# A mixture-of-experts trunk layer on one Trainium2 core: TensorE's sequencer is told of the next expert's far body in every near body

## What is computed

```python
def grouped_moe(h, router_w, router_b, w_gate, w_up, w_down):
    t = h.reshape(-1, D)
    logits = (t @ router_w).astype(jnp.float32) + router_b
    aff = jax.nn.softmax(logits, axis=-1)
    ...                      # best group of four experts, top 2 inside it
    for e in range(N_EXPERTS):                       # 16
        hid = jax.nn.silu(t @ w_gate[e]) * (t @ w_up[e])     # 2048 -> 1024
        y = y + combine[:, e:e + 1] * (hid @ w_down[e])      # 1024 -> 2048
```

## Time and profile before

| what | value |
| --- | --- |
| median of 3 runs | 1832.25 us (1832.04 to 1832.47) |
| the profiled execution: its own time | 1831.08 us |
| the profiled execution: its span | 1829.4 us |
| mean granted TensorE clock over the span | 0.978 |
| the experts' part | from about 815 us to about 1805 us of the span |

### The profile page before, as it was taken

How to read it: one execution, slowest core, us unless ns; L and a number is a source line. 1 busy time by engine, 2 the same in 40 slices (tenths; PEclk the granted TensorE clock), 3 DMA queues, 4 the chain that set the end, 5 groups by cost and what they waited for, 6 DMA issues and landing times.

```text
span 1829.4 us, 22863 instructions
## 1 busy us (share of the span) xinstructions
PE 1696.8 (93%) x9430; PEld 1001.4 (55%) x9430; DVE 610.4 (33%) x1082; ACT 186.0 (10%) x439; POOL 362.6 (20%) x161
## 2 busy tenths in 40 slices
PE   6889998999999999969999989999988989899996
PEld 5668887878888878654443233343423324334322
DVE  0453648687676342441121120211111111211114
ACT  0000112100001100041010010010100101001000
POOL 0014740167677768300000000000000000000000
PEclk9889999999999999989999999999999999999999
DMA  9996886486788744434689998999999999899995
GB/s 386 425 388 176 366 365 256 190 332 287 316 352 341 303 165 203 184 140 185 277 368 418 428 425 373 427 425 427 427 427 428 427 428 428 359 428 423 429 427 215
DMA packets 51015, 629.92 MB, mean 344 GB/s; under 512 B 5775, under 2 KB 8240, under 8 KB 11848
## 3 DMA queue, kind: packets, MB, share of 16 engines
q1 hardware_dynamic: 49768, 623.15, 82.1%
q10 hardware_dynamic: 1120, 5.00, 0.7%
HBM read 624.46 MB, written 3.67 MB: 343 GB/s over the span
## 4 chain that ended last, share of the span: by engine, by line
PE 71%; DMA 19%; DVE 6%; SPq 1%; issue 1%; ACT 0%; DVEq 0%; ACTq 0%
PE bank L1396 24%; PE bank L858 20%; PE bank L870 9%; DMA ring<-in_w_up_gate 7%; PE bank L1158 7%; DMA region_g<-in_w_up_gate 6%; PE bank L1234 4%; PE bank L829 3%; DMA ring<-in_w_down 3%; PE bank L882 2%; DVE ada_rows L1912 2%; DMA region_g<-in_w_down 2%; DMA ring<-in_w_in 1%; PE bank L877 1%; SPq L584 1%
## 5 line engine op out<-in xcount | busy, mean ns | idle before, releaser
L858 PE MATMUL bank<-ring,region_b 128*64 128x512 f32 x1792 | 409.9, 604 | 42.2 <-DMA ring<-in_w_up_gate 34.5
L729 POOL TENSOR_TENSOR ring<-ring 128x1024 f32<-128x1024 f32 x152 | 360.2, 2396 | 356.4 <-DMA ring<-in_w_in 237.4
L858 PEld LDWEIGHTS bank<-ring,region_b 128*64 128x64 f32 x1792 | 124.5, 138 | 296.4 <-issue 244.8
L870 PE MATMUL bank<-ring,region_f 128*64 128x512 f32 (+1 forms) x1408 | 231.7, 518 | 8.9 <-DMA ring<-in_w_down 8.9
L1396 PE MATMUL bank<-ring,region_a 128*128 128x256 f32 x768 | 174.3, 385 | 4.7 <-DVE region_c L2106 4.2
L1396 PE MATMUL bank<-ring,region_x 128*128 128x256 f32 x768 | 170.2, 379 | 0.0
L1396 PEld LDWEIGHTS bank<-ring,region_a 128*128 128x128 f32 x768 | 147.7, 193 | 27.8 <-issue 6.9
L870 PEld LDWEIGHTS bank<-ring,region_f 128*64 128x64 f32 (+1 forms) x1408 | 77.0, 127 | 145.7 <-issue 116.9
L1396 PEld LDWEIGHTS bank<-ring,region_x 128*128 128x128 f32 x768 | 145.6, 190 | 19.3
L2339 DVE TENSOR_TENSOR region_a<-bank,region_a 128x512 f32<-128x512 f32 x128 | 79.5, 683 | 199.2 <-PE bank L882 199.1
L1912 DVE SCALAR_TENSOR_TENSOR bank<-ring,condT,bank 128x512 f32<-128x512 f32 x190 | 143.4, 755 | 5.7
(11 more groups left out here) (233 smaller groups left out, 1304.8 us busy)
## 6 DMA issues: line engine op xcount, KB each, us to landing
ring<-in_w_up_gate SPq DMA_DIRECT2D x112, 2048.0 KB, 22.2
ring<-in_w_down SPq DMA_DIRECT2D x56, 2048.0 KB, 20.8
ring<-in_ada_w SPq DMA_DIRECT2D x44, 2048.0 KB, 11.8
ring<-in_w_in SPq DMA_DIRECT2D x31, 2048.0 KB, 13.7
region_g<-in_w_up_gate SPq DMA_DIRECT2D x16, 2048.0 KB, 26.0
ring<-in_w_branch SPq DMA_DIRECT2D x8, 2048.0 KB, 14.6
ring<-in_w_out SPq DMA_DIRECT2D x8, 2048.0 KB, 9.8
region_g<-in_w_down SPq DMA_DIRECT2D x8, 2048.0 KB, 19.3
```

The lines of the kernel that those rows point to most:

```text
L729: ins = pool.tensor_tensor(quarter(s, *out)[:, k:k + 4, :], quarter(s, *in0)[:, k:k + 4, :], quarter(s, *in1)[:, k:k + 4, :], op)
L858: last = nc.tensor.matmul(bank_of(x, j)[n * c:n * c + n, 0:2 * m], tokens(x, 8 * half + k), w[:, k % 4, :, m * c:m * c + m], start=(half = ...
L870: last = nc.tensor.matmul(bank_of(x, q)[n * c:n * c + n, 0:m], hidT[x][:, k, :], w[:, k % 4, m * c:m * c + m], start=(k == 0), stop=(k == ...
```

## The change

An announcement is now emitted in the small body of *every* expert but the last, at the same place in the body, and every branch into a large body but the first is tied to the one in the small body ahead of it:

```diff
@@ -1131,8 +1131,8 @@
                 extra("F")(x)
                 if len(xs) > 2:
                     extra("add F")(x)
-            if not xs and le == GRP - 1 and not last_turn:
-                large_announced[g + 1] = pe.mark_branch_hint_location()
+            if not xs and ne < NE - 1:
+                large_announced[ne + 1] = pe.mark_branch_hint_location()
             down(0, 1, first).then_inc(half_used, 1)
             if 0 < len(xs) < 3:
                 extra("add F")(1)
@@ -1533,7 +1533,7 @@
                         e = expert_at(g, le)
                         count = pe.value_load(counts[0:1, e:e + 1], min_val=0, max_val=T)
                         here = few_tokens(pe, f"pe{g}_{le}", count, lambda xs: expert_pe(pe, mm, g, le, xs),
-                                          large_announced.get(g) if le == 0 else None)
+                                          large_announced[g * GRP + le])
                         asked.append((g, le, count, here))
```

## The result

| | kernel before | changed kernel |
| --- | --- | --- |
| median of 7 runs each | 1832.04 us (1829.18 to 1832.64) | 1840.75 us (1835.44 to 1841.93) |
| ratio | | 1.0049 (95% interval 1.0040 to 1.0058) |
| the profiled execution: its own time | 1831.08 us | 1840.70 us |
| its span | 1829.4 us | 1839.0 us |
| fetches on queue 8 | 88 | 98 |

The change makes the kernel slower, by 8.7 us or 0.5%. The forecast was 1.5 us slower, within what can be told from no change, and a range that ended at 1836.3. The measured time lies outside it.

A forecast was written before the change was run, and what follows sets the result against it. Weights set the pace in three stretches, TensorE between them. Nine unused announcements' fetches added 0.8, 0.3 and 0.3 us, other terms about nothing: 1832.25 + 1.5 = 1833.8 us, range 1831.5 to 1836.3 for 8 in 10.

The forecast's parts named there:

- What bounds the kernel, and which jumps are taken: Weights set the pace in three stretches, TensorE between them; large bodies run only at ne 0, 4 and 12, all announced.
- (a): The announcement instruction in nine small bodies, 31 ns each: cost 0, hidden by queued matmuls; 0.3 us without that cover.
- (b): The branch not taken after each of nine unused announcements: 9 ns each, 0.1 us in all.
- (c): Nine extra fetches on queue 8, 0.16 us each on average where the weights set the pace: 1.4 to 1.5 us.
- the three stretches: 971 to 1091, 1205 to 1571 and 1690 to 1799 us, where the DMA engines are always busy and weights set the pace.
- steps that show only when a fetch hits the latest part: In the weight queue, a fetch delays one parallel part, showing only if that part is already latest; 0 to 4.5 us.
- the pieces: Timed parts of the long stretch, 1344 to 1570.7 us; their weight transfers together fell behind by 1.5 us over nine fetches.
- The block that comes next: Rival: an unused announcement pushes out the following block, stalling 4.5 us at ends of ne 1, 5 or 13; chance 0.06.
- Moved: Later branches and large bodies: a spoiled announcement is covered at ne 4 and 12, costs 4.5 us on ways back; taken as 0.
- The "slower" rivals: A lost next block, 4.5 us per stall at ne 1, 5, 13 (chance 0.06); full steps in three stretches, +4.5 us (0.05).

The follow-up runs named there:

- the kernel at slot 88: The changed kernel with its expert code started at slot 88 instead of 100, so large bodies stand as in the kernel before; ratio 1.0010 against the kernel before.
- second try with two announcements: The changed kernel with a second unused announcement 33 instructions ahead of the first in each small body that runs; ratio 1.0018 against the kernel before.
- the last kernel: The changed kernel with ne 0's large body for two or more extra blocks laid right behind the second branch; 1827.12 us, ratio 0.9989 against the kernel before.

## Why the prediction was wrong

**What bounds the kernel, and which jumps are taken: right.** Only ne 0, 4 and 12 run large bodies, all three were announced before, and L775 had the same long executions after.

**(a) and (b), the instruction and the untaken branch: right.** Twelve executions of 31 to 36 ns, the other branches at 68 to 85 ns. With the way back in its old slot (start at slot 88) ne 0 and ne 1 took 107.1 and 51.2 us, for 107.1 and 51.3 before.

**(c), the fetch: the total was right, in part by luck.** The prediction had said that more than nine new fetches would make (c) wrong. Ten came, and the tenth is the shift's, as the runs without added announcements show. Nine at 0.16 us were to cost 1.5 us. The profile of the kernel at slot 88 has 1.2 us more, and its ratio says 1.8 (-0.2 to 3.7). But the split was off: 0.8, 0.3 and 0.3 us over the three stretches were forecast, and about 1.5, 0 and 0 came. That is 0.3 us for each announcement where it showed, twice the price, and nothing elsewhere; the two errors made up for each other. The prediction's reading, steps that show only when a fetch hits the latest part, would do that, and no run shows it. The price has a slip too: 68.59 / 14 is 4.899 us for a transfer, so that the pieces lost 0.10, 0.74 and 0.55 us, 1.4 in all and not 1.5. And that fetches caused this was assumed.

**The block that comes next isn't lost.** No small body after an unused announcement began late: ne 2 and 3 came through L775 in 85 and 73 ns. Each unused announcement made one fetch more (97 for 88), not two. The Trainium skill, "Runtime: NRT & Kernel Launch", section "Instruction fetch mechanics", says that the instruction memory is "only 2 cache lines"; that a far block would then push out the next one was the prediction's working, and isn't what TensorE did here. The Trainium skill's other rule in that section, that a taken branch whose target is out of the window must wait for its target, is what L789, L775 and L798 show, at 4.1 to 6.2 us.

**The step that failed is "Moved".** It says: "On a way back from a large body there is no such cover and it would cost 4.5 us. I take 0." The mechanism was named and the price was nearly right (3.9 us of wait), but the term was put at nothing without a reason. What was missing was the place. The text looked only at how far the *branches* and *bodies* move, not at where the ways back stand. One of them stood four slots short of the edge of its block, so twelve more instructions were sure to push it over. That much is arithmetic on the compiled program, and needs no run; what a jump pays behind the edge needed the runs. Then the lower clock behind a wait of 4.6 us adds 1.7 us, by the same matmuls' 5.35 for 3.65 us, which the earlier trace rows had shown for other waits. Together 5.6 us were missing from the sum of 1.5, and 7.2 is what the profiles of the experts' part show.

The "slower" rivals had the right size, 4.5 us for a stall without cover, and put it at the wrong mechanism: a block pushed out, at the ends of ne 1, 5 and 13.

## What to carry to other kernels

An edit that costs nothing where it stands can cost microseconds where it pushes something else: after adding or removing instructions ahead of far code, work out in which slot of its fetch block every taken jump stands, and keep the announced ones clear of the first slots (20 was too early here, 56 was not). Test it with the same shift made of instructions that never run. And an announcement is of use only for a jump that is taken and whose wait nothing covers; each unused one makes a fetch on the same DMA engines that carry the weights. Where one far jump is sure to be taken, its target can be laid next to it: that took L798's place here in 82 ns, where announcing it left 3297.

## What the runs showed of the hardware

- An announced jump fetches its target when its block is entered, as far as four slots tell: it took 4.1 to 4.3 us at slot 8, 2.4 at slot 20, 0.3 at slot 56 and at slot 252, and the fetch started 1.6 to 1.9 us after the jump at slot 8, with it at slot 20, and 5.8 us ahead of it at slot 56. An announcement made 100 us earlier, from another block, didn't bring that forward.
- A later announcement that follows at once replaces an earlier one: the jumps into ne 4 and 12 went from 0.35 to 6.1 and 6.2 us.
- An unannounced far jump took 4.7 to 5.1 us where the DMA engines were nearly idle (8 GB/s), with two fetches, and 5.9 to 6.2 us where the weights kept them busy (426 GB/s). With one fetch the closing jump took 3.3 to 3.8 us.
- At the way back of ne 0 the clock fell after idle times of 4.6 and 4.8 us, and sixteen matmuls took 1.7 us longer; after 2.7 us, in the same place, it didn't. The length of one wait doesn't decide it. It also fell to 0.50 after waits of 2.46 us (second try with two announcements, at 1402.9 us) and 2.14 us (the last kernel, at 1518.3 us), both behind waits of 1.2, 1.2 and 0.6 us earlier in the same expert.
